# Softmax of two heads at once in the second mixer, and wide scores a step earlier in the first

## The reference

```python
def mla_mixer(...):                      # 8 heads; x: 256 tokens, c: 256 context tokens
    s = einsum('bhqd,bhkd->bhqk', qn, kn) + einsum('bhqr,bkr->bhqk', qr, kr)   # 128 and 64 rows deep
    p_x, p_c = joint_softmax(scores(qn, qr_rot, kn_x, kr_x_rot), scores(qn, qr_pl, kn_c, kr_c))
    return pv(p_x, v_x) + pv(p_c, v_c)   # and the same for the context's own queries

def swa_mixer(...):                      # 16 heads of 64, 4 key heads, window of 128
    s_w = where(valid, einsum('bkgqd,bkjd->bkgqj', q_rot, k_b) * scale, NEG_INF)
    s_c = ctx_scores(q_pl)
    p_w, p_c, _ = joint_softmax(s_w, s_c, sink)    # the sink takes a share and has no value
    return pv(p_w, v_b) + pv(p_c, v_c)
```

## Time and profile before

| | us |
|---|---|
| median of 3 runs | 2864.19 |
| lowest, highest | 2854.37, 2866.15 |
| the profiled execution | 2856.93 |
| its span in the trace | 2855.1 |
| busy: TensorE, VectorE, ScalarE | 2663.7, 1565.7, 1078.3 |
| mean granted clock of TensorE | 0.974 |

### The profile page before, as it was taken

How to read it: one execution, slowest core, us unless ns; L and a number is a source line. 1 busy time by engine, 2 the same in 40 slices (tenths; PEclk the granted TensorE clock), 3 DMA queues, 4 the chain that set the end, 5 groups by cost and what they waited for, 6 DMA issues and landing times.

```text
span 2855.1 us, 44372 instructions
## 1 busy us (share of the span) xinstructions
PE 2663.7 (93%) x17820; PEld 2325.0 (81%) x17820; DVE 1565.7 (55%) x2307; ACT 1078.3 (38%) x1427; POOL 0.2 (0%) x4
## 2 busy tenths in 40 slices
PE   7999999999999969999998999999999999887997
PEld 6887899888789968877786688787888778876997
DVE  7676665677666564333366553333353423676665
ACT  3354553335455443222241433222232222345443
POOL 0000000000000000000000000000000000000000
PEclk9999999999999989999999999999999999999998
DMA  7655567564557734344432024354534444531563
GB/s 212 198 165 192 177 210 215 154 193 156 188 167 222 213 105 122 106 132 128 133 96 74 1 60 126 106 144 114 145 98 125 139 116 112 114 80 53 144 188 103
DMA packets 591271, 394.54 MB, mean 138 GB/s; under 512 B 52278, under 2 KB 584660, under 8 KB 590932
## 3 DMA queue, kind: packets, MB, share of 16 engines
q1 hardware_dynamic: 591060, 391.63, 47.9%
HBM read 390.54 MB, written 1.05 MB: 137 GB/s over the span
## 4 chain that ended last, share of the span: by engine, by line
PE 76%; DVE 13%; ACT 5%; issue 3%; DMA 2%; DVEq 0%; SPq 0%; ACTq 0%
PE bank L2044 76%; DVE w_lo L1205 4%; ACT w_hi L853 3%; DMA raw<-in_ffn_w_out 2%; DVE xs L1220 1%; DVE t L1220 1%; DVE t L1217 1%; DVE small L1839 1%; DVE h_lo L1220 1%; DVE gates L1213 0%; ACT xs L857 0%; ACT t L857 0%; DVE acc L1213 0%; ACT x_hi L857 0%; DMA raw<-in_w_in 0%
## 5 line engine op out<-in xcount | busy, mean ns | idle before, releaser
L1205 DVE TENSOR_TENSOR w_lo<-raw,w_hi 128x2048 fp32r<-128x2048 f32 (+3 forms) x337 | 687.3, 2040 | 575.8 <-ACT w_hi L853 573.8
L853 ACT CAST w_hi<-raw 128x2048 fp32r<-128x2048 f32 (+3 forms) x337 | 572.9, 1701 | 771.0 <-PE bank L2044 386.7
L2044 PE MATMUL bank<-h_hi,w_hi 128*128 128x512 f32 (+1 forms) x1688 | 590.5, 350 | 25.9 <-DVE h_lo L1220 14.2
L2044 PE MATMUL bank<-h_lo,w_hi 128*128 128x512 f32 (+1 forms) x1688 | 583.1, 345 | 0.0
L2044 PE MATMUL bank<-h_hi,w_lo 128*128 128x512 f32 (+1 forms) x1688 | 582.2, 345 | 0.0
L2044 PE MATMUL bank<-x_hi,w_hi 128*128 128x256 f32 x1344 | 387.8, 289 | 35.8 <-DVE x_lo L1220 13.1
L2044 PEld LDWEIGHTS bank<-h_hi,w_hi 128*128 128x128 f32 x1688 | 321.1, 190 | 79.5 <-issue 23.3
L2044 PE MATMUL bank<-x_lo,w_hi 128*128 128x256 f32 x1344 | 378.8, 282 | 0.0
L2044 PE MATMUL bank<-x_hi,w_lo 128*128 128x256 f32 x1344 | 378.3, 281 | 0.0
L2044 PEld LDWEIGHTS bank<-h_hi,w_lo 128*128 128x128 f32 x1688 | 321.1, 190 | 39.0
L2044 PEld LDWEIGHTS bank<-h_lo,w_hi 128*128 128x128 f32 x1688 | 321.4, 190 | 37.6
(11 more groups left out here) (282 smaller groups left out, 3622.8 us busy)
## 6 DMA issues: line engine op xcount, KB each, us to landing
raw<-in_ffn_w_in SPq DMA_DIRECT2D x176, 512.0 KB
raw<-in_ffn_w_out SPq DMA_DIRECT2D x64, 704.0 KB
raw<-in_w_in SPq DMA_DIRECT2D x40, 1024.0 KB
xs<-in_mod_w SPq DMA_DIRECT2D x36, 1024.0 KB, 7.3
raw<-in_mod_w SPq DMA_DIRECT2D x36, 1024.0 KB
raw<-in_w_ff_in SPq DMA_DIRECT2D x32, 1024.0 KB
raw<-in_w_ff_out SPq DMA_DIRECT2D x32, 1024.0 KB
raw<-in_w_out SPq DMA_DIRECT2D x8, 1024.0 KB
```

The costliest lines, as they stand in the source:

```text
L853: act.copy(w_hi[s][:, w], raw[at % SLOTS][:, w]).then_inc(hi_made, c.did(hi_made))
L1205: dve.tensor_tensor(w_lo[s][:, w], raw[r][:, w], w_hi[s][:, w].bitcast(F32), ALU.subtract).then_inc(lo_made, c.did(lo_made))
L2044: ins = pe.transpose(o, l, r) if transpose else pe.matmul(o, l, r, start=start, stop=stop)
```

## The change

In the second mixer VectorE now works on pairs. `highest_pair(s)` does mask and maximum for units s and s+1 and then one minimum on two columns; `scaled_pair(s)` does one sum and one reciprocal on two columns and then the two weights. The first is called at even steps, the second at the odd step that follows. ScalarE does the two exponentials of a pair and then the two sink exponentials, at even steps. `stat` is used per pair.

In the first mixer TensorE's `score` loses the products of the 128-row part (`kn,qn`) for parts 0 and 1; the new `early` issues them, after the transpose at the odd step before, with the claim of the two banks. Other instructions are the same.

```diff
--- before.py
+++ after.py
@@ -1110,17 +1110,25 @@
                     if 2 <= s < len(units) + 2:
                         act.wait_ge(turn_full, c.next(turn_full))
                         do(ACT.Copy, t2[:, s % 2, :], bank[2][:, :]).then_inc(turned, c.did(turned))
-                    if s < len(units):
+                    if s < len(units) and with_sink:
+                        if s % 2 == 0:
+                            act.wait_ge(logits_ready, c.next(logits_ready))
+                            st = stat[s // 2 % 3]
+                            act.wait_ge(c.last, c.own())
+                            for x in range(2):
+                                do(ACT.Exp, prob[(s + x) % 3], score_banks[(s + x) % 4][:, :], bias=st[:, 2 + x:3 + x], scale=scale,
+                                   accum_out=st[:, 4 + x:5 + x]).then_inc(a_step, c.did(a_step))
+                            for x in range(2):
+                                h = units[s + x][0]
+                                signal = exp_made if x else a_step
+                                do(ACT.Exp, st[:, 6 + x:7 + x], sink[:, h:h + 1], bias=st[:, 2 + x:3 + x]).then_inc(signal, c.did(signal))
+                    elif s < len(units):
                         act.wait_ge(logits_ready, c.next(logits_ready))
                         st, L, b = stat[s % 3], prob[s % 3], score_banks[s % 4]
                         h, part = units[s]
                         if part < 2:
                             act.wait_ge(c.last, c.own())
-                            signal = a_step if with_sink else exp_made
-                            do(ACT.Exp, L, b[:, :], bias=st[:, 2:3], scale=scale, accum_out=st[:, 4:5]).then_inc(signal, c.did(signal))
-                            if with_sink:
-                                act.wait_ge(c.last, c.own())
-                                do(ACT.Exp, st[:, 5:6], sink[:, h:h + 1], bias=st[:, 2:3]).then_inc(exp_made, c.did(exp_made))
+                            do(ACT.Exp, L, b[:, :], bias=st[:, 2:3], scale=scale, accum_out=st[:, 4:5]).then_inc(exp_made, c.did(exp_made))
                         else:
                             for q in range(2):
                                 act.wait_ge(c.last, c.own())
@@ -1825,37 +1833,61 @@
 
             def soft_attention(units, scale, hi, lo_part, ends, with_sink, meanwhile=None):
 
+                def highest_pair(s):
+
+                    st, pair = stat[s // 2 % 3], units[s:s + 2]
+                    for x, (h, part) in enumerate(pair):
+                        b = score_banks[(s + x) % 4]
+                        far = slice(P - P * part, 2 * P - P * part)
+                        dve.wait_ge(s_full, c.next(s_full))
+                        dve.wait_ge(c.last, c.own())
+                        tt(b[:, far], b[:, far], win_mask[:, S * part + far.start:S * part + far.stop], ALU.add).then_inc(v_step, c.did(v_step))
+                        dve.wait_ge(c.last, c.own())
+                        dve.tensor_reduce(st[:, x:x + 1], b[:, :], AX.X, ALU.max).then_inc(v_step, c.did(v_step))
+                    t, _ = swa_place(pair[0][0])
+                    dve.wait_ge(c.last, c.own())
+                    stt(st[:, 2:4], st[:, 0:2], -scale, nsink[:, :].rearrange("p (a x t) -> p a x t", a=2, x=2)[:, t // 4, :, t % 4],
+                        ALU.mult, ALU.min).then_inc(logits_ready, c.did(logits_ready))
+
+                def scaled_pair(s):
+
+                    st = stat[s // 2 % 3]
+                    dve.wait_ge(exp_made, c.next(exp_made))
+                    dve.wait_ge(c.last, c.own())
+                    tt(st[:, 4:6], st[:, 4:6], st[:, 6:8], ALU.add).then_inc(v_step, c.did(v_step))
+                    dve.wait_ge(c.last, c.own())
+                    recip(st[:, 0:2], st[:, 4:6]).then_inc(s_free, c.did(s_free, 2))
+                    dve.wait_ge(c.last, c.own())
+                    for x in range(2):
+                        L = prob[(s + x) % 3]
+                        ts(L, L, st[:, x:x + 1], None, ALU.mult).then_inc(weights_ready, c.did(weights_ready))
+
                 for s in range(len(units) + 4):
-                    if s < len(units):
+                    if s < len(units) and with_sink:
+                        if s % 2 == 0:
+                            highest_pair(s)
+                    elif s < len(units):
                         h, part = units[s]
                         st, b = stat[s % 3], score_banks[s % 4]
                         dve.wait_ge(s_full, c.next(s_full))
-                        if with_sink:
-                            far = slice(P - P * part, 2 * P - P * part)
-                            dve.wait_ge(c.last, c.own())
-                            tt(b[:, far], b[:, far], win_mask[:, S * part + far.start:S * part + far.stop], ALU.add).then_inc(v_step, c.did(v_step))
                         dve.wait_ge(c.last, c.own())
                         if part < 2:
                             dve.tensor_reduce(st[:, 0:1], b[:, :], AX.X, ALU.max).then_inc(v_step, c.did(v_step))
-                            if with_sink:
-                                dve.wait_ge(c.last, c.own())
-                                stt(st[:, 2:3], st[:, 0:1], -scale, nsink[:, h:h + 1], ALU.mult, ALU.min).then_inc(logits_ready, c.did(logits_ready))
-                            else:
-                                dve.wait_ge(c.last, c.own())
-                                ts(st[:, 2:3], st[:, 0:1], -scale, None, ALU.mult).then_inc(logits_ready, c.did(logits_ready))
+                            dve.wait_ge(c.last, c.own())
+                            ts(st[:, 2:3], st[:, 0:1], -scale, None, ALU.mult).then_inc(logits_ready, c.did(logits_ready))
                         else:
                             dve.tensor_reduce(st[:, 0:2], pair(b[:, :]), AX.X, ALU.max).then_inc(v_step, c.did(v_step))
                             dve.wait_ge(c.last, c.own())
                             ts(st[:, 2:4], st[:, 0:2], -scale, None, ALU.mult).then_inc(logits_ready, c.did(logits_ready))
                     if meanwhile is not None:
                         meanwhile(s)
-                    if 1 <= s <= len(units):
+                    if with_sink:
+                        if s < len(units) and s % 2 == 1:
+                            scaled_pair(s - 1)
+                    elif 1 <= s <= len(units):
                         st, L = stat[(s - 1) % 3], prob[(s - 1) % 3]
                         dve.wait_ge(exp_made, c.next(exp_made))
                         if units[s - 1][1] < 2:
-                            if with_sink:
-                                dve.wait_ge(c.last, c.own())
-                                tt(st[:, 4:5], st[:, 4:5], st[:, 5:6], ALU.add).then_inc(v_step, c.did(v_step))
                             dve.wait_ge(c.last, c.own())
                             recip(st[:, 6:7], st[:, 4:5]).then_inc(s_free, c.did(s_free))
                             dve.wait_ge(c.last, c.own())
@@ -2506,7 +2538,7 @@
                 for j, src in enumerate(srcs):
                     mm(b[:, S * j:S * j + S], rot, src, True, True, give if j == len(srcs) - 1 else None)
 
-            def soft_attention(units, score, weigh, paired, meanwhile=None):
+            def soft_attention(units, score, weigh, paired, meanwhile=None, early=None):
 
                 pe.wait_ge(ra.free, ra.all_used())
                 rs4 = Ring(c, score_banks, s_full, s_free)
@@ -2525,7 +2557,12 @@
 
                 for s in range(n + 3):
                     if s < n and s % 2 == 0:
-                        score([claim(rs4), claim(rs4)], units[s:s + 2])
+                        if early is None:
+                            banks = [claim(rs4), claim(rs4)]
+                        elif s == 0:
+                            banks = [claim(rs4), claim(rs4)]
+                            early(banks, units[s:s + 2])
+                        score(banks, units[s:s + 2])
                     if meanwhile is not None:
                         meanwhile(s)
                     if s == 3:
@@ -2539,6 +2576,9 @@
                     else:
                         if 2 <= s < n + 2:
                             turn(s - 2)
+                        if early is not None and s % 2 == 1 and s + 1 < n:
+                            banks = [claim(rs4), claim(rs4)]
+                            early(banks, units[s + 1:s + 3])
                         if s >= 3:
                             pe.wait_ge(turned, c.value(turned, rt2.used)) if s < n + 2 else pe.wait_ge(rt2.free, rt2.all_used())
                             weigh(t2[:, (s - 3) % 2, :], *units[s - 3])
@@ -2603,8 +2643,6 @@
                     both = [(b, h, slice(HALF * (h % 2), HALF * (h % 2) + HALF)) for b, (h, _) in zip(banks, pair)]
                     if part < 2:
                         toks = slice(P * part, P * part + P)
-                        for b, h, _ in both:
-                            mm(b[:, :], qn[:, h, toks], kn[:, h, :], True, False)
```

(9 more changed lines are left out.)

## The result

| | before | changed |
|---|---|---|
| median of 8 runs each, us | 2865.98 | 2878.62 |
| lowest, highest | 2854.37, 2870.63 | 2866.93, 2883.95 |
| profiled execution, span | 2855.1 | 2877.1 |

A forecast was written before the change was run, and what follows sets the result against it. VectorE was taken to pace the second attention, TensorE the first. Terms 11.4 + 1.8 + 1.5 + 0 = 14.7 us gave 2872 from the profiled execution, 2879 from the median; forecast 2877, 8-in-10 range 2865 to 2892.

The forecast's parts named there:

- VectorE sets the pace of the second attention: Second mixer's attention before the change: VectorE takes 2.30 us a unit, and TensorE's transposes wait for it.
- What is removed: Second mixer, VectorE: 9 operations a pair instead of 12, saving 0.66 us a pair, 10.6 us over 16 pairs.
- What is added: Second mixer: VectorE's sum waits openly for the exponentials, 1.9 us a pair; a pair lasts 5.68 us against 4.60.
- The stage up to the last weights: Second attention, from unit 2's mask to the last weights: 88.3 us against 76.9, so +11.4 us.
- The end: End of the second attention: the last two transposes share one bank and one moment, +1.8 us.
- The clock: TensorE in the second attention: 4 to 12 low-clock spells of 0 to 0.4 us each, taken as +1.5 us.
- The first mixer: First mixer's attention: moved wide score products leave the time from pair to pair unchanged, 0 us.
- The signs: Profile after: sum idles 1.9 us a pair, pairs 5.7 or 6.2 us, second attention's granted clock below 0.91.
- pairing pays: Rival, second mixer: exponentials are ready when the sum comes up, -13 us, 2849 us; chance 0.05.
- First mixer gains: Rival, first mixer: moved wide products close TensorE's gaps, -5.3 us, total +10, 2872 us; chance 0.13.
- Moved scores cost: Rival, first mixer: TensorE changes between 128-row and 64-row weights elsewhere, +2 to +4 us on top, 2881; chance 0.05.
- The clock stays low through most of the stage: Rival, second attention: low TensorE clock makes pairs 7.1 us against 5.95, +32 us in all, 2894 us; chance 0.13.

The follow-up runs named there:

- order-alone run: Changed kernel's order kept, but minimum, sum and reciprocal done for each unit apart, against the changed kernel; second attention 103.6 us against 94.2, no ratio.
- second-part-alone run: Only the second mixer's paired softmax, first mixer's scores as before, against the kernel before; ratio 1.0055, second attention 96.4 us.

## Why the prediction was right

It said 2877 us and slower; it was 2878.6. The mechanism was right, and the nearness of the two times is in part luck. The forecast of 2877 stands on 2862 us for the kernel before, which came out at 2866 over 8 runs, 3.7 higher, and the change cost 12.6 us by the medians where 14.7 were forecast, 2.1 less. The chances also had more above half a percent (0.55) than below (0.42). The median fell below, at 0.43%, and the interval does not decide it. By its steps:

- **VectorE sets the pace of the second attention.** Right: in the changed kernel and in four variants the stage follows VectorE's chain with its waits.
- **What is removed.** 0.66 us a pair by distances between starts, 10.6 us in all. The order-alone run gives 0.51 a pair: too large by a quarter. It did no harm, since the pair of 5.68 us was added up from its own distances and not from this saving.
- **What is added.** 1.9 us of open wait a pair; measured 1.88. A pair 5.68; measured 5.69, and 11.89 for four units as computed.
- **The stage up to the last weights.** +11.4 us; measured 88.9 instead of 76.9, +12.0, of which 0.42 is the slow spell and 0.19 a pair whose weights came that much late, once, for a reason not traced.
- **The end.** +1.8 us; measured +1.8.
- **The clock.** I took +1.5 us for the low clock beside both terms, on 4 to 12 spells of 0 to 0.4 us each. There were three spells in the body, as many as before, though TensorE was idle for 35.6 us of the stage instead of 24.2; one cost 0.42 us and the others nothing. The term was too large by 1.1 us in this trace. It also counted twice: it took off the 2.6 us of waits of the kernel before, which are already in the 76.9 us that the +11.4 are measured from. And it left out the end: the second-part-alone run had a spell over the uncovered end and paid 2.7 us. The stage came out at +13.8 against 14.7.
- **The first mixer.** 0; measured -0.2 us, and 1.0006 alone.
- **The signs.** The granted clock of the stage was to fall below 0.91; it fell from 0.94 to 0.91, with single stretches of 20 us from 1.00 to 0.77. The pairs were to last 5.7 or 6.2 us, and all of the 14 but two did.

The rivals: "pairing pays" needed a wait under 0.66 us and had 1.88. "First mixer gains" would have needed products in the gaps, which the run with the first wide product ahead of the transpose showed to be one position away. "Moved scores cost" left no mark (81.2 us alone against 81.1). "The clock stays low through most of the stage" did not happen: the granted clock was low in three spells, and they cost 0.42 us together.

VectorE did not step past the waiting sum. It stood still for the 1.88 us up to 2562.70, although TensorE had finished the next pair's scores at 2561.42, and did that pair's masks only afterwards. The Trainium skill says the same of its queue, strict FIFO ("TensorE: Matmul & The Clock Gate", Part 1), and this trace agrees. The row that the prediction names for it, the sum at 2556.95 in the kernel before, does not show it: there the next pair's scores ended at 2557.56, so no mask was ready during that wait.

## What to carry to other kernels

Merging small operations of two work items saved 0.17 us an operation on VectorE here, but it moves the signal to the other engine behind the second item's work and takes away the work that lay under the answer; count both before merging, and keep one item of lag between request and use. A whole pair of lag took the wait away but left 3.3 us more behind the last sum (7.6 against 4.3), and gained little over one unit of lag. When a product is moved to fill a gap, look on which side of the waiting instruction it lands: two places that read alike differed by 3.4 us. When a stage gets slower, look at its uncovered end as well as its period.

## What was not expected of the hardware

- The same instructions gave a stage of 94.2, 94.1 and 96.4 us in three executions, by where TensorE's half-clock spells fell: 0.42 us or nothing in the body, 2.7 us at the end. In the kernel before each of three spells in the body cost 0.78 us, the 0.88 us at the sum less the usual 0.10.
- In the changed kernel the granted clock was 1.00 from 2560 to 2580, though TensorE stood still some 1.9 us in each pair, and 0.77 from 2600 to 2620 with the same pattern of work.
- Two weight operations on 512 columns without a wait between them took 0.88 us together, 0.40 from start to start, less than the 0.48 of one.
